# The first gather of a mixture-of-experts round, parted into two of 64 rows with one expert each

## The reference, cut to what matters

```python
def hierarchical_moe(h, w_group, b_group, w_expert, b_expert, w_gate, w_up, w_down):
    ht = h.reshape(-1, D)                       # 512 x 1024
    gp = jax.nn.softmax(ht @ w_group + b_group)
    p_top, g_idx = lax.top_k(gp, 1)             # one group of 4
    ...
    top_l, e_idx = lax.top_k(el_sel, TOP_K)     # two experts of its 8
    ...
    def expert_step(acc, p):
        wg, wu, wd, ge = p                      # 1024x256, 1024x256, 256x1024
        z = jax.nn.silu(ht @ wg) * (ht @ wu)
        return acc + ge[:, None] * (z @ wd), None
```

## Time and profile before

| | us |
|---|---|
| median of 3 executions | 1242.36 (1239.82 to 1242.53) |
| the profiled execution | 1240.7 |
| its span | 1238.9 |
| mixture of layer 0, first transposes to last product on PE | 518.6 to 737.6 |
| mixture of layer 1, the same | 989.6 to 1208.6 |
| TensorE busy | 1128.2 (91% of the span) |
| DMA | 274.57 MB, mean 222 GB/s |

### The profile page before, as it was taken

The page is one execution under the profiler, slowest core; times in us unless marked ns, Lnnn a source line. Parts: engine busy times, 40 slices in busy tenths (PEclk is TensorE's granted clock), DMA queues, the critical chain, the costliest instruction groups (busy, mean ns, idle before and its releaser), DMA issues.

```text
span 1238.9 us, 29223 instructions
## 1 busy us (share of the span) xinstructions
PE 1128.2 (91%) x12462; PEld 622.5 (50%) x12462; DVE 521.1 (42%) x964; ACT 419.4 (34%) x815; POOL 214.3 (17%) x245
## 2 busy tenths in 40 slices
PE   6999999999999999899998876999999899998880
PEld 5455555555555644555554434544554455554440
DVE  5756555564665411511110105799941511111105
ACT  5335445444454421311111113555443321111112
POOL 2000000000000000222221110688800222222110
PEclk9999999999999989899998987999999899999995
DMA  4011101011012168799999996216502899999996
GB/s 159 3 54 62 40 21 58 4 57 41 20 58 85 59 248 332 258 406 423 426 423 426 425 385 252 93 68 249 244 0 74 318 352 423 425 425 424 425 381 240
DMA packets 51923, 274.57 MB, mean 222 GB/s; under 512 B 14900, under 2 KB 17076, under 8 KB 34642
## 3 DMA queue, kind: packets, MB, share of 16 engines
q1 hardware_dynamic: 39184, 243.28, 48.9%
q0 software_dynamic: 10880, 21.00, 4.5%
q10 hardware_dynamic: 1728, 8.42, 1.8%
HBM read 266.36 MB, written 23.07 MB: 234 GB/s over the span
## 4 chain that ended last, share of the span: by engine, by line
PE 78%; DMA 11%; ACT 4%; DVE 3%; issue 2%; SPq 2%; ACTq 0%; POOLq 0%; DVEq 0%
PE psum L944 14%; PE psum L1504 14%; PE psum L2034 9%; PE psum L2312 8%; DMA big<-in_moe_w_gate_up_dram 7%; PE psum L957 7%; PE psum L1685 6%; DMA big<-in_moe_w_down_dram 2%; PE psum L911 2%; PE psum L1808 1%; PE psum L2322 1%; PE psum L2290 1%; PE psum L526 1%; PE psum L1834 1%; ACT big L1867 1%
## 5 line engine op out<-in xcount | busy, mean ns | idle before, releaser
L944 PE MATMUL psum<-big 128*64 128x256 f32 x1536 | 191.6, 393 | 21.2 <-issue 12.9
L1504 PE MATMUL psum<-big 128*128 128x512 f32 x384 | 191.0, 618 | 5.5 <-ACT big L1555 4.3
L944 PEld LDWEIGHTS psum<-big 128*64 128x64 f32 x1536 | 107.2, 139 | 89.2 <-issue 30.6
L1030 DVE SCALAR_TENSOR_TENSOR big<-psum,big 128x128 f32<-128x128 f32 x64 | 22.5, 351 | 304.9 <-ACT big L987 304.9
L957 PE MATMUL psum<-big 128*64 128x512 f32 x512 | 120.9, 593 | 2.1 <-DMA big<-in_moe_w_down_dram 1.5
L871 POOL DMA_INDIRECT chosen<-big x64 | 63.7, 996 | 330.3 <-ACT big L998 177.2
L2034 PE MATMUL psum<-big 128*128 128x512 f32 x256 | 116.3, 607 | 0.8 <-ACT big L2417 0.8
L1877 ACT COPY big<-psum 128x512 f32<-128x512 f32 (+1 forms) x112 | 68.4, 649 | 113.6 <-PE psum L1685 111.7
L2262 POOL TENSOR_TENSOR big<-big 128x512 f32<-128x512 f32 x76 | 96.7, 1273 | 34.3 <-ACT big L2399 24.1
L847 POOL DMA_DIRECT2D rows<-h x8 | 4.7, 582 | 555.6 <-DVE h L2073 555.6
L2312 PE MATMUL psum<-big,conv_w 128*128 128x512 f32 x224 | 96.5, 592 | 0.0
(11 more groups left out here) (273 smaller groups left out, 1355.9 us busy)
## 6 DMA issues: line engine op xcount, KB each, us to landing
big<-in_moe_w_gate_up_dram SPq DMA_DIRECT2D x40, 2048.0 KB
big<-in_moe_w_down_dram SPq DMA_DIRECT2D x64, 1024.0 KB
conv_w<-in_moe_w_gate_up_dram SPq DMA_DIRECT2D x8, 2048.0 KB
h<-in_moe_w_gate_up_dram SPq DMA_DIRECT2D x8, 2048.0 KB
big<-in_moe_w_gate_up_dram SPq DMA_DIRECT2D x16, 1024.0 KB, 38.4
big<-in_rwkv_w_rkv_dram SPq DMA_DIRECT2D x24, 512.0 KB, 4.3
conv_w<-in_conv_w_pw_dram SPq DMA_DIRECT2D x8, 1024.0 KB, 4.8
big<-chosen ACTq DMA_DIRECT2D x6, 1024.0 KB, 9.3
```

What stands on the lines that cost most here:

```text
L944: last = nc.tensor.matmul(o[half * SLOTS:(half + 1) * SLOTS, 0:F_EXP].rearrange("p (u f) -> p u f", u=2), m.xT[e // 2 % 2][:, c, (e % 2) * ...
L1504: last = nc.tensor.matmul(bank[b], m.w[:, n, c, :], x[:, c, :], start=(c == 0), stop=(c == C - 1))
```

## The change

Four things are changed in each round; the rest of the diff is a semaphore that is replaced to make one free.

- The first gather is issued as two of 64 rows, one for the slots of expert 0 (partitions 0 to 63) and one for those of expert 1 (partitions 64 to 127), each with a semaphore of its own. The row numbers of expert 1 for this come from one new DVE instruction, ahead of those that write `gather_at`.
- TensorE transposes the rows of expert 0 (eight transposes of 64 rows into bank 0), runs all of `gate_up(0)`, and then transposes the rows of expert 1 (eight more, into bank 1).
- VectorE takes one bank for each expert, again 128x512 numbers in each of two instructions.
- `gate_up(0)` no longer waits in its middle, and `gate_up(1)` waits for the second of these DVE instructions.

```diff
@@ class Moe
+                self.gather_second = m.take(1)
@@ dve_tables
             dve.wait_ge(m.slot_step, S * r + 2)
+            nc.vector.scalar_tensor_tensor(out=m.gather_second[0:SLOTS].bitcast(i32), in0=number[0:SLOTS, 1:2], scalar=-1.0,
+                                           in1=m.far[0:SLOTS, 1:2], op0=ALU.add, op1=ALU.add)
@@ pool_moe
+                def gather_half(half):
+                    at = m.gather_second if half else m.gather_at[:, 0:1]
+                    nc.gpsimd.indirect_dma_start(
+                        m.x[0][half * SLOTS:(half + 1) * SLOTS], None, rows[m.layer],
+                        bass.IndirectOffsetOnAxis(ap=at[0:SLOTS].bitcast(u32), axis=0),
+                        bounds_check=T - 1, oob_is_err=False).then_inc(m.x_in[0] if half else m.first_rows_in, 16)
-                for p in range(4):
+                for half in range(2):
+                    gather_half(half)
+                for p in range(1, 4):
                     gather(p)
@@ pe_moe
+                def first_columns(half):
+                    if half:
+                        pe.wait_ge(m.x_in[0], 16 * (N_PAIRS // 2) * r + 16)
+                    else:
+                        pe.wait_ge(m.first_rows_in, 16 * r + 16)
+                    s = slice(half * SLOTS, (half + 1) * SLOTS)
+                    wide = m.x[0][s].rearrange("p (f c) -> p c f", c=C)
+                    if half == 0:
+                        pe.wait_ge(m.xT_ready, ROWS_A_ROUND * r + FREE1)
+                    pe.sem_inc(pe_tick)
+                    for c in range(C):
+                        last = nc.tensor.transpose(bank[half][:, c * SLOTS:(c + 1) * SLOTS], wide[:, c, :], ident[s, s])
+                    last.then_inc(m.xT_in_psum, 1)
@@ gate_up
-                    if e % 2 == 0:
+                    if e % 2 == 0 or e == 1:
                         pe.wait_ge(m.xT_ready, ROWS_A_ROUND * r + (FREE1 + (rows_of(e // 2) if e else 1)))
...
-                            else:
-                                pe.wait_ge(m.xT_ready, ROWS_A_ROUND * r + (FREE1 + rows_of(0)))
@@ the round on TensorE
-                columns(0)
+                first_columns(0)
                 gate_up(0)
+                first_columns(1)
@@ dve_moe
+                def take_first_rows(half):
+                    dve.wait_ge(m.xT_in_psum, ROWS_A_ROUND * r + half + 1)
+                    nc.vector.tensor_tensor(
+                        m.xT[0][:, :, half * SLOTS:(half + 1) * SLOTS], bank[half].rearrange("p (c s) -> p c s", s=SLOTS),
+                        m.g_col.unsqueeze(2).broadcast_to([P, C, SLOTS]), ALU.mult).then_inc(m.xT_ready, 1)
...
-                take_rows(0)
+                for half in range(2):
+                    take_first_rows(half)
```

More of the change, by code:

```diff
@@ L279, in __init__ @@
                 self.last_in = sem("last_in" + s)
+                self.first_rows_in = sem("first_rows_in" + s)
                 self.xT_in_psum = sem("xT_in_psum" + s)
@@ L291, in __init__ @@
                 self.back_in = [Turn(tile_rows_in[t], 16 * (1 + layer)) for t in range(TT)]
-                self.first_pick_in = sem("first_pick_in" + s)
                 self.h_step = sem("h_step" + s)
@@ L421, in sp_return_h @@
             sp.wait_ge(m.gate_up_done, FREE2 - 2 + UPS_A_ROUND * rounds)
-            sp.dma_start(h, rows[m.layer].rearrange("(t p) d -> p t d", p=P)).then_inc(m.first_pick_in, 16)
+            sp.dma_start(h, rows[m.layer].rearrange("(t p) d -> p t d", p=P)).then_inc(m.first_pick_in.sem, 16)
         def sp_load_both(m, sp, e):
@@ L911, in columns @@
                         last = nc.tensor.transpose(bank[c // 4][:, (c % 4) * P:(c % 4 + 1) * P], wide[:, c, :], ident[:])
-                        if p == 0 and c == C // 2 - 1:
-                            last.then_inc(m.xT_in_psum, 1)
                     last.then_inc(m.xT_in_psum, 1)
@@ L1012, in take_rows @@
                 def take_rows(p):
-                    def weigh(first, end):
-                        return nc.vector.tensor_tensor(
-                            m.xT[p % 2][:, first:end, :], psum[:, first * P:end * P].rearrange("p (c s) -> p c s", s=P),
-                            m.g_col[:, first:end].unsqueeze(2).broadcast_to([P, end - first, P]), ALU.mult)
-                    if p == 0:
-                        for half in range(2):
-                            dve.wait_ge(m.xT_in_psum, ROWS_A_ROUND * r + half + 1)
-                            weigh(half * C // 2, (half + 1) * C // 2).then_inc(m.xT_ready, 1)
-                    else:
-                        dve.wait_ge(m.xT_in_psum, ROWS_A_ROUND * r + rows_of(p))
-                        weigh(0, C).then_inc(m.xT_ready, 1)
+                    dve.wait_ge(m.xT_in_psum, ROWS_A_ROUND * r + rows_of(p))
+                    nc.vector.tensor_tensor(
+                        m.xT[p % 2], psum[:, 0:C * P].rearrange("p (c s) -> p c s", s=P),
+                        m.g_col.unsqueeze(2).broadcast_to([P, C, P]), ALU.mult).then_inc(m.xT_ready, 1)
+                def take_first_rows(half):
+                    dve.wait_ge(m.xT_in_psum, ROWS_A_ROUND * r + half + 1)
+                    nc.vector.tensor_tensor(
+                        m.xT[0][:, :, half * SLOTS:(half + 1) * SLOTS], bank[half].rearrange("p (c s) -> p c s", s=SLOTS),
+                        m.g_col.unsqueeze(2).broadcast_to([P, C, SLOTS]), ALU.mult).then_inc(m.xT_ready, 1)
                 def gated(e):
@@ L1050, in act_load_back @@
             act.wait_ge(m.round_done, rounds + 1)
-            act.dma_start(m.back[0][:, 0:D], back[0][:, 0:D]).then_inc(m.first_pick_in, 16)
+            act.dma_start(m.back[0][:, 0:D], back[0][:, 0:D]).then_inc(m.first_pick_in.sem, 16)
             act.dma_start(m.back[0][:, D:], back[0][:, D:]).then_inc(m.back_in[0].sem, 16)
@@ L1059, in dve_combine @@
                 if t == 0 and k == 0:
-                    dve.wait_ge(m.first_pick_in, 32)
+                    dve.wait_ge(m.first_pick_in.sem, m.first_pick_in.by(32))
                 if k or t:
@@ L2226, in bass_hybrid_rwkv7_conformer_hmoe @@
             m_.hn_ready = Turn(mixer_.mixed, 0)
+        moe[0].first_pick_in, moe[1].first_pick_in = Turn(rw.wk_in, 16 * PAIRS), Turn(rw.wr_in, 16 * PAIRS)
         def sp_conv_w1(m, sp, q, b):
```

2 lines of the change are left out of this document (1 added, 1 removed).

## The result

The changed kernel takes 1246.39 us (median of 13 runs, 1241.96 to 1251.97), the kernel before 1242.1 us beside it (13 runs, 1237.74 to 1246.34). The ratio is 1.0042 with an interval of 1.0024 to 1.0060. The time is inside the range of 1241.0 to 1248.0 us, but the likeliest case, no change, did not come out: the kernel is slower by more than 0.2%, and by about twice the 2.1 us of the sum.

A forecast was written before the change was run, and what follows sets the result against it. Each mixture was taken to end with its weight stream: the stream's start plus its volume over 424 GB/s. Per layer 0 + 0.45 + 0.2 + 0.4 = 1.05 us, 2.1 us in all, gave 1242.36 + 2.1 = 1244.5 us, range 1241.0 to 1248.0.

The forecast's parts named there:

- the likeliest case, no change: Whole kernel: a shift within 2.5 us (0.2%), likeliest time 1244.5 us; same had 0.52, slower 0.41, faster 0.07.
- the sum: Whole kernel: 0 + 0.45 + 0.2 + 0.4 = 1.05 us per layer, 2.1 us in two layers.
- forecast 0.45: Round's start: VectorE starts behind eight transposes instead of four, no cheaper at 64 columns; 0.45 us a layer.
- forecast 2.10: Behind gate_up(0): second transposes, VectorE's weighing and handovers lie bare, delaying gate_up(1) by 1.16 + 0.03 + 0.69 + 0.22 us.
- The late gather's 0.4: Weight stream: gather 2's 0.25 MB, released later, fall into the stream; 0.4 us a layer, between 0 and 0.6.
- the leak of 0.2: Weight stream: queue covers the late third half load with 0.9 us over; 0.2 us a layer taken, bounds 0 and 2.10.
- the clock falls: Rival, round's start: pauses behind transposes halve TensorE's clock; some 1.7 us a layer, up to 1247.9 us; chance 0.04.
- rows and warm-up end together: Before the first transposes: gathered rows and warm-up end within 0.15 us, so earlier rows gain at most 0.05 us.
- The stream runs thin: Rival, weight stream: DMA idles until the late third half load flows; in full 2.95 us a layer, 1248.3 us; chance 0.37.
- Its half case: Weight stream: half of the PE delay reaches it, (0.45 + 0.4 + 1.05) x 2 = 3.8 us, or 1246.2 us.
- The rows decide after all: Rival, round's start: the landing decides, half a gather lands 1.2 us sooner; -0.15 us a layer, 1242.1 us; chance 0.09.
- the clock rival: Round's start: TensorE's clock drops to 1.2 GHz if transposes do not count as work; up to 5.5 us; chance 0.04.

The follow-up runs named there:

- order alone: The kernel after with one gather of 128 rows and without the new DVE instruction, so only the new TensorE and VectorE order: 1246.3 us, ratio 1.0040.
- pauses filled: One idle 128x512 product behind each set of transposes: on the kernel after 1244.8 us, ratio 1.0019; on the new order with one 128-row gather 1244.72 us, 1.0028.
- the delay alone: The kernel before with two idle 128x512 products (1.7 us) between gate_up(0) and the second pair's transposes in each layer: 1242.19 us, ratio 1.0008.
- the gather alone: The kernel before with the gather of pair 2 held back until gate_up(0) is done, TensorE's order untouched: 1242.12 us, ratio 1.0008.
- the repeat: The kernel after, unchanged, run once more for a second profile: 1249.61 us (6 runs), ratio 1.0063.
- before's repeat: The kernel before, unchanged, run once more for a second profile: one run of 1241.72 us.

## Why the prediction was right in its range and wrong in its case

All fourteen profiles together, two mixtures each:

| order | falls | from T to the end without a fall, us | with a fall, us |
|---|---|---|---|
| before's, untouched or with the longer warm-up | 0 of 6 | 218.85 to 219.31 | none |
| before's with a delay of TensorE or of a gather | 2 of 6 | 219.91 to 221.08 | 221.07, 221.27 |
| before's, parted gathers | 1 of 2 | 219.16 | 221.66 |
| the new, pauses open (after twice, order alone) | 4 of 6 | 219.99, 221.21 | 221.52 to 223.65 |
| the new, pauses filled | 2 of 4 | 219.72, 220.60 | 222.15, 222.63 |
| the second set ahead or in the middle | 2 of 4 | 220.61, 220.90 | 221.47, 221.93 |

*The sum of 1.05 us a layer held roughly, as a whole.* Without a fall the new order's four mixtures average 220.38 us. Seven of the order of before (its first row, and the one of the parted gathers) average 219.09. The difference is 1.3 us a layer, 2.6 us in all against the forecast 2.1. Its terms: from T to the product of expert 0 it is 2.02 to 2.07 us where before has 1.66, so +0.4 (forecast 0.45); that row of eight narrow transposes takes 1.07 to 1.12 us against 1.16, no half price. From the product of expert 0 to that of expert 1 it is 2.90 us instead of 1.02, so +1.9 (forecast 2.10). The late gather's 0.4 and the leak of 0.2 are too small together: from the first half load to expert 30 the kernel after has 201.72 and 201.02 us without a fall against 200.16, so about 1.2 us, with the pauses filled 0.8, where the sum has 0.6. The two are not told apart; the delay alone and the gather alone each come to some 0.5 us a layer by the middle of their ratios, with 0 in both intervals.

*The step that failed is "the clock falls": it was given 0.04, and the new order fell in four mixtures of six.* The prediction has it in the sentence "But 16 transposes of 1.94 us and a pause stand from 761.75 us, and the stretch behind them has the clock 1.00". These transposes had no wait ahead of them; the first of a round have. Open pauses without a long wait ahead brought no fall in two mixtures: layer 0 of the repeat, with no wait, and layer 1 of the kernel after, behind 0.77 us. The price is less sure. With the new order's pauses open, the columns of the table give 222.7 us in the mean against 220.6, so 2.1 us a mixture, but from four mixtures and two. What rows show directly is the first half load: it comes 5.4 to 5.8 us behind T where it takes 4.0 without a fall (one fall that began late: 4.85), 1.4 us later in the mean. In two of the four falls the third half load comes 0.8 to 0.9 us later still behind the first (7.49 and 7.42 us, where 6.58 is usual). I had at most 1.7 us, "part of which would reach the stream". With before's order the price is anything from none to 2.5 us: the kernel with the late gather has 221.07 us with a fall in layer 0 and 221.08 without one in layer 1.

*Behind that stands the reading that rows and warm-up end together.* "An earlier landing finds TensorE busy" was read from one execution. Over the profiles six warm-up MATMULs take 2.82 us at full clock, 4.52 where the clock rises on the way (the kernel after in layer 0: 0.50 from 512.0 to 515.4 us, over at 516.1), and 5.25 to 5.47 where nearly all of them run at half clock (before in layer 0: 0.50 from 513.4 to 516.8 us, 0.56 to 518.6); the transposes start 3.4 to 6.3 us behind the gather's issue (7.0 where both halves are waited for). Only where both are long do they meet. Elsewhere TensorE waits, in before's kernel too. Of all 28 mixtures, the eleven falls came behind waits of 1.0 to 3.1 us; behind shorter ones there is none, and behind waits of 1.0 us or more there are five without one. The new order, pauses open, fell behind all four such waits. The kernels with before's order and one gather fell behind two of five. So wait and pause together may be worse than the wait alone, but three things leave the pauses' part open. The filled pauses fell behind both of their waits. The kernel with the second set in the middle, whose first pause of 0.96 us is open, kept the clock behind a wait of 1.49 us. And the warm-up's own clock goes with the falls as well: behind a warm-up of 4.5 us or more, much of it at half clock, and a wait of 1.0 us or more, nine of eleven mixtures fell, behind one of 2.82 us at full clock two of five (waits of 2.00 and 3.06 us fell, 1.24, 1.49 and 2.27 did not). That is the reverse of what the expectation of before's repeat said, a fall only behind a warm-up at full clock. The new order had such slow warm-ups ahead of three of its four waits, the order of before with one gather ahead of three of five. Why the change makes falls more frequent is not shown. That they were more frequent rests on 4 of 6 against 2 of 12 mixtures and on the timed clocks.

Each timed execution has a mean granted clock on record, and these agree. It is 0.9703 over the 19 of the kernel after and 0.9729 over the 92 of before that were timed beside the experiments, and in the first 13 of the kernel after the slower executions are those with the lower clock (correlation -0.79). With the pauses filled it is 0.9726 on the kernel after, but on the order alone 0.9716 goes only to 0.9722. The clock is not the whole loss either: it is lowest, 0.969, with the second set ahead or in the middle, and these lose less than the kernel after.

*The bill.* Six mixtures of the new order with open pauses average 222.0 us from T to the end, the six of before's order in the table's first row 219.1: 2.9 us a layer. The rows split it at the first half load. From T to there it is 4.95 us in the mean against 3.63, so 1.3 us: 0.4 for the transposes, and 0.9 for the falls (1.4 us in four of six). From there to expert 30 it is 1.6 us (201.73 against 200.16), where the sum had 0.6: 1.2 of it without a fall, the rest in the mixtures that fell. That makes 5.9 us in two layers; 0.42% of 1242.1 is 5.2, with 3.0 to 7.5 as its interval. So the miss has two parts, the falls and a stream term that was too small. How large each is, so few mixtures say only roughly.

*The rivals.* "The stream runs thin" (0.37) has the sign and the size of the result by another road. Its third half load is late by 1.9 us; when produced alone (1.7 us) that costs about 0.5 us a layer by the timed ratio and 1.2 by the one profile, and in full it would have been 2.1. Its half case gave 1246.2 us beside the measured 1246.39, with a stretch behind the first half load that is 1.45 us longer a layer where the profiles have 1.6; but it had no fall ahead of it, so part of that agreement is luck. "The rows decide after all" (0.09) is half right: the rows do decide when the warm-up is short. But half a gather is hardly sooner. Where TensorE waited for rows in layer 1, 128 rows came 3.86, 4.61, 5.45 and 5.68 us behind the issue, and 64 rows 3.39, 3.58, 4.11 and 5.51: 0.75 us less in the mean (4.90 and 4.15), with a spread three times that. In layer 0 it is nothing: 4.77 to 6.28 us with 128 rows (mean of seven 5.75), 5.45 to 6.27 with 64 (mean of four 5.89). The POOL instruction is hardly shorter with half the rows, 966 to 1044 ns:

```profile
L930 PEld LDWEIGHTS psum<-ident,big x32: 182/202/206, 518.1 to 998.4; 64*128 64x128 f32 x32
...
L863 POOL DMA_INDIRECT big<-rows,big x4: 966/1000/1044, 511.9 to 990.0; - x4
```

*The rules of the Trainium skill.* The first row above settles the weight load: 64 rows by 128 columns load in 202 ns at the median, and the 128 rows by 128 columns of before's L911 in 194, so half the rows save nothing. The Trainium skill says so (TensorE: Matmul & The Clock Gate, LDWEIGHTS (loading the stationary operand)), and the trace agrees on the rows. The columns alone do not give the time here, since the same 128 take 137 ns in the flips. That transposes do not count as activity for the clock (the same page of the Trainium skill, Part 4: PE-mode transpose) was my road to the clock rival. The runs neither confirm it nor rule it out: layer 0 of the repeat, with eight transposes, 0.96 us of pause, the product and eight more transposes, kept the clock, so transposes and pause were not enough by themselves. The eleven falls all had a wait of 1.0 us or more ahead of the transposes.

## What to carry to other kernels

Where a stage starts behind a transfer, look at the granted clock and at the wait ahead of it in several executions, not in one. A warm-up of a fixed number of products ran for 2.8, 4.5 or 5.4 us here, as the clock stood, and "both end together" may be an accident. An edit that puts short pauses behind such a wait should be priced with a fall of the clock as a case of its own, above all where its first product releases a saturated stream. Split a loss at the point where the stream is released: here about 1.3 us a layer lay ahead of it and 1.6 behind it, and one cause would have explained only one of them. And a split that brings half of the data sooner pays only if nothing then waits twice for it. Here the second half's way through TensorE, VectorE and back lay bare between two products, 1.9 us for a start that came hardly sooner.

## What the runs showed of the hardware that was not expected

The same six MATMULs of the warm-up took 2.82, 4.52 or 5.25 to 5.47 us within otherwise equal executions, by the clock granted while they ran. A gather of 64 rows costs POOL 966 to 1044 ns as one of 128 costs 0.99 to 1.12 us, and splitting one therefore adds a full microsecond on POOL. From a gather's issue to the transposes it took 4.8 to 6.3 us in layer 0 and 3.4 to 5.7 in layer 1; in the kernel after the DMA moves 419 GB/s in the stretch where the first gather is issued in layer 0, and in layer 1:

```profile
988.50:991.20 2.70, 2.70 (x11) 0.99 (x6) 1.56 (x9) 0.31 (x2) 2.00 (x2) 1.00 0.60 232
```

There the engines have room, and the same row has the warm-up at the full clock. That a busier DMA makes the landing later is what these two stretches suggest; no run separated it.
